# Heads of q and k turned by VectorE block transposes, stored in another column order and scaled by ScalarE

## The chip, the cores and the metric

The program runs on one core of a Trainium2 chip. The metric is the device time of one execution in microseconds (us), lower is better; the median of three runs stands for the kernel. The core has a matrix engine (PE, TensorE), a vector engine (DVE), a scalar engine (ACT), a general engine (POOL, GpSimd) and a queue engine (SP, SyncE) that only issues transfers. Each runs its own list of instructions in order and waits for others by semaphores.

## The reference, cut to what matters

Three layers stand one behind the other: a retention layer, a chunked attention layer and a mix of pooling and latent attention, on 1024 positions of width 1024. The change touches the second one:

```python
def chunked_attention_mixer(h, w_in, q_g, k_g, rel_table, w_out):
    proj = h @ w_in                                # 1024 x 8192: q, k, v, g, 16 heads of 128 each
    q, k, v, g = jnp.split(proj, 4, axis=-1)
    q = rms_norm_f32(q.reshape(B, S, 16, 128), q_g)   # norm over the 128 of a head
    k = rms_norm_f32(k.reshape(B, S, 16, 128), k_g)
    ...
    s = jnp.einsum('bqhd,bkhd->bhqk', q_j, k_j) * scale + bias    # 64 queries, 576 keys
    p = jax.nn.softmax(s, axis=-1)
    return jnp.einsum('bhqk,bkhd->bqhd', p.astype(v.dtype), v_j)
```

The scores contract over the 128 of a head, so PE wants q and k of a head with the head dimension on the partitions (turned), while the projection h @ w_in leaves positions on the partitions.

## The kernel before, in words

**Products.** All large products are float32 and are made of three passes of a rounded format (high by high, low by high, high by low; `product`, lines 1182 to 1184). The weights therefore pass a ring of RING = 4 slots: a raw tile in SBUF, then ACT copies its high part (`hi`, line 1813, into `w_hi`), then POOL subtracts to get the low part (line 1068, `w_lo`), then PE uses both. `hi(n)` waits until PE is done with slot n - 4, so at best it stands three slots ahead of its use.

**Blocks.** The input projection of the attention layer is cut in 16 blocks, numbers 12 to 27, and each block is computed with seven products (Strassen's scheme), whose left and right factors are sums. DVE forms the weight sums (`wide_sum` line 2386, raw sums line 2368) and adds the products from PSUM into four quadrants c11, c22, c21, c12 of the block (`wide_evict`, line 2406; `evict`). The buffers of the quadrants are called c11, u3 (c22), m1s (c21) and u2 (c12); names with _k are those of the second block of a pair. Blocks 19, 21, 23, 25 are q and each is computed together with the k block behind it (20, 22, 24, 26) as a "wide" pair: a slot of theirs feeds 256 columns of both and a product has four slots, in the order 0, 3, 1, 4, 5, 2, 6. Block 27 is v, not wide, with two slots in a product. So a wide pair is followed by a wide pair three times, and by block 27 once.

**Norm of q and k.** Behind each quadrant of a pair (128 x 1024 for q and as much for k) DVE squares (line 2470), reduces to 8 sums (line 2471), ACT takes the root (line 1892), DVE inverts (line 2477) and scales the whole buffer by one multiplication (`unit_scale`, line 2479). SP then stores it, one transfer of 512 KB with rows of 1 KB (line 687), to `blk` in HBM, positions by columns. The buffers are used again by the next pair: ACT's `m1s_copy` (line 1883) waits for the stores of c21, DVE's eviction u2 for those of c12.

**Attention.** It works in tiles e = 8 h + i (head h, 128 queries i). SP loads q, k and v of a head in runs of 512 B (`a_load`, line 964). PE turns q and k, four pieces of four 128 x 128 tiles to a head (`a_turn_head`, lines 1368 to 1377, at the tiles listed in `A_TURN_AT`; the four pieces of head 0 stand at product 5 of block 27), into PSUM; ACT writes the high part with the gain multiplied in (line 2105), DVE the low part (line 2841). Per tile PE computes scores (`a_scores`), turns the probabilities (`a_turn`, line 1522, ACT copies them out by lines 2132 to 2135) and multiplies by v (`a_values`, line 1534); DVE takes maxima, ACT the exponentials, DVE the inverse sum, POOL multiplies by it (line 1134). The stage runs from about 1484 us to 1760 us.

## Time and profile before

| | |
|---|---|
| median of 3 runs | 2449.77 us (2449.53 to 2451.17) |
| the profiled execution | 2450.25 us, its span 2448.4 us |
| mean granted TensorE clock | 0.999 |
| busy share PE, DVE, ACT, POOL | 99%, 64%, 45%, 50% |

The span is the stretch from the first to the last instruction on the chip. Where a row gives a start time, it is counted from the start of the span. Shares are means over all stages, which have different loads.

### The profile page before, as it was taken

Reading aid. Unit: us, or ns where it says so; the run is one execution under the profiler, and the core shown is the slowest. Engines: PE = TensorE matmul, PEld = TensorE weight load, DVE = VectorE, ACT = ScalarE, POOL = GpSimd, SP = SyncE. Lnnn points to the kernel's source line nnn. Section 1 sums busy time; section 2 is a strip of 40 time slices with the busy share of each in tenths; the row PEclk is TensorE's granted clock in tenths of the full one; section 3 lists DMA queues with packets and bytes.
Section 4 is the critical chain, followed back from the end, with each engine's and each line's share of the span. In section 5 each row is a group of like instructions: output and inputs, shape, how many; then the busy total and the mean of one; then the engine's idle time right before and its main releaser. Section 6 shows DMA issues by size and latency. Waiting matters only on the chain.

```text
span 2448.4 us, 36045 instructions
## 1 busy us (share of the span) xinstructions
PE 2419.0 (99%) x13808; PEld 2076.6 (85%) x13808; DVE 1578.4 (64%) x2151; ACT 1105.7 (45%) x2052; POOL 1235.7 (50%) x883
## 2 busy tenths in 40 slices
PE   7999999999999999999999999999999999999999
PEld 6888898875588898899888899999988888788887
DVE  6965657588543386653766766666434489788863
ACT  5322223344544353322322226777534434888861
POOL 1645545430044455545555555555454445866664
PEclk9999999999999999999999999999999999999999
DMA  7554544493034345543332257454144343300034
GB/s 277 157 190 154 180 163 158 142 325 137 27 112 156 104 150 181 176 142 107 122 116 98 89 166 226 124 156 121 50 135 158 105 161 123 103 1 1 2 127 156
DMA packets 241196, 329.21 MB, mean 134 GB/s; under 512 B 19401, under 2 KB 173825, under 8 KB 239233
## 3 DMA queue, kind: packets, MB, share of 16 engines
q1 hardware_dynamic: 239552, 326.80, 40.3%
q8 instruction: 111, 1.82, 0.3%
q14 instruction: 61, 0.49, 0.1%
q10 hardware_dynamic: 1472, 0.10, 0.0%
HBM read 247.53 MB, written 79.33 MB: 133 GB/s over the span
## 4 chain that ended last, share of the span: by engine, by line
PE 91%; DVE 5%; issue 2%; ACT 1%; POOL 1%; DMA 1%; SPq 0%; DVEq 0%; ACTq 0%
PE ps L1182 23%; PE ps L1184 23%; PE ps L1183 23%; PE ps L1534 4%; PE ps L1707 2%; PE ps L1522 2%; PE ps L1688 2%; PE ps L1451 2%; PE ps L1470 2%; PE ps L1464 1%; DVE s_raw L2349 1%; PE ps L1375 1%; PE ps L1202 1%; PE ps L1434 1%; PE ps L1407 1%
## 5 line engine op out<-in xcount | busy, mean ns | idle before, releaser
L1068 POOL TENSOR_TENSOR w_lo<-raw,w_hi 128x512 fp32r<-128x512 f32 (+1 forms) x452 | 652.9, 1453 | 794.4 <-ACT w_hi L1813 758.8
L1813 ACT ACTIVATE w_hi<-raw 128x512 fp32r<-128x512 f32 (+1 forms) x456 | 282.9, 629 | 795.1 <-PE ps L1184 633.4
L1182 PE MATMUL ps<-w_hi,s_hi 128*128 128x256 f32 (+2 forms) x832 | 262.8, 316 | 0.8 <-POOL w_lo L1068 0.3
L1183 PE MATMUL ps<-w_lo,s_hi 128*128 128x256 f32 (+2 forms) x832 | 262.0, 315 | 0.0
L1184 PE MATMUL ps<-w_hi,s_lo 128*128 128x256 f32 (+2 forms) x832 | 262.0, 315 | 0.0
L1068 POOL TENSOR_TENSOR w_lo<-raw_wide,w_hi 128x512 fp32r<-128x512 f32 x112 | 174.0, 1560 | 131.3 <-ACT w_hi L1813 131.3
L2462 DVE TENSOR_TENSOR u<-u,ps 128x1024 f32<-128x1024 f32 (+1 forms) x96 | 116.4, 1212 | 148.9 <-PE ps L1184 145.5
L1182 PE MATMUL ps<-w_hi,a_hi 128*128 128x256 f32 (+2 forms) x624 | 196.7, 315 | 0.0
L1183 PE MATMUL ps<-w_lo,a_hi 128*128 128x256 f32 (+2 forms) x624 | 196.6, 315 | 0.0
L1184 PE MATMUL ps<-w_hi,a_lo 128*128 128x256 f32 (+2 forms) x624 | 196.5, 315 | 0.0
L1182 PE MATMUL ps<-s_hi,w_hi 128*128 128x512 f32 x480 | 188.6, 393 | 3.2 <-DVE s_lo L2336 2.3
L1134 POOL TENSOR_TENSOR a_p<-a_p,st 128x640 f32<-128x640 f32 (+4 forms) x128 | 130.7, 1027 | 117.9 <-DVE st L2880 117.7
L1184 PE MATMUL ps<-s_hi,w_lo 128*128 128x512 f32 x480 | 186.9, 389 | 0.0
L1183 PE MATMUL ps<-s_lo,w_hi 128*128 128x512 f32 x480 | 186.8, 389 | 0.0
L2368 DVE TENSOR_TENSOR raw<-raw 128x1024 f32<-128x1024 f32 (+1 forms) x96 | 134.5, 1401 | 58.4 <-DMA raw<-in_w 56.3
L1182 PEld LDWEIGHTS ps<-w_hi,s_hi 128*128 128x128 f32 x832 | 158.5, 191 | 12.7 <-issue 2.2
L1184 PEld LDWEIGHTS ps<-w_hi,s_lo 128*128 128x128 f32 x832 | 158.6, 191 | 10.0
L1183 PEld LDWEIGHTS ps<-w_lo,s_hi 128*128 128x128 f32 x832 | 158.6, 191 | 9.9
L1813 ACT ACTIVATE w_hi<-raw_wide 128x512 fp32r<-128x512 f32 x112 | 70.5, 633 | 195.9 <-PE ps L1184 177.7
L1162 POOL TENSOR_TENSOR l_p<-l_p,st 128x1024 f32<-128x1024 f32 x64 | 121.3, 1895 | 72.9 <-DVE st L3056 71.8
L1182 PE MATMUL ps<-a_hi,w_hi 128*128 128x512 f32 x360 | 141.7, 393 | 0.0
L1183 PE MATMUL ps<-a_lo,w_hi 128*128 128x512 f32 x360 | 140.9, 391 | 0.0
(341 smaller groups left out, 6214.6 us busy)
## 6 DMA issues: line engine op xcount, KB each, us to landing
raw<-in_w SPq DMA_DIRECT2D x159, 512.0 KB, 4.3
ada_c<-in_ada SPq DMA_DIRECT2D x14, 2304.0 KB, 10.8
blk<-u SPq DMA_DIRECT2D x54, 512.0 KB, 4.0
raw_wide<-in_w SPq DMA_DIRECT2D x32, 512.0 KB, 4.6
blk<-c SPq DMA_DIRECT2D x27, 512.0 KB, 3.4
blk<-m1s SPq DMA_DIRECT2D x27, 512.0 KB, 3.3
ada_first<-in_ada SPq DMA_DIRECT2D x12, 768.0 KB, 16.0
r_g<-blk SPq DMA_DIRECT2D x8, 1024.0 KB, 9.4
```

Of the source, the lines that this page charges most:

```text
L1068: pool.tensor_tensor(w_ring(w_lo, n), w_source(n), w_ring(w_hi, n).bitcast(F32), ALU.subtract)\
L1134: pool.tensor_tensor(a_p[:, e % 4, 0:w], a_p[:, e % 4, 0:w], st[:, 172 + e % 4:173 + e % 4].to_broadcast([P, w]), ALU.mult).then_inc(a_pro ...
L1162: pool.tensor_tensor(l_p[e % 3][:, :], l_p[e % 3][:, :], st[:, 136 + e % 4:137 + e % 4].to_broadcast([P, S]), ALU.mult)\
L1182: pe.matmul(out, a_hi_, b_hi_, start=first, stop=False, skip_group_check=True)
L1183: pe.matmul(out, a_hi_, b_lo_, start=False, stop=False, skip_group_check=True)
L1184: return pe.matmul(out, a_lo_, b_hi_, start=False, stop=last, skip_group_check=True)
L1451: mm = pe.matmul(ps[:, 2 + k], r_kd[r_kept(e) % 2][:, k * P:(k + 1) * P], r_v[h % 2][:, i], start=(i != 1), stop=(i != 0))
L1470: mm = pe.matmul(ps[:, 4 + e % 2], r_q[h % 2][:, k, i * P:(i + 1) * P], r_state_at[b % 2][:, k], start=False, stop=(k == 1))
L1534: mm = pe.matmul(ps[:, 6 + i // 4, (i % 4) * P:(i % 4 + 1) * P], a_v[h % 4][:, j], a_pT[:, e % 2, c * P:(c + 1) * P], start=(c == 0), stop ...
L1813: act.activation(w_ring(w_hi, n), w_source(n), ACT.Copy).then_inc(w_rounded, 1)
L2368: dve.tensor_tensor(raw_quad(dst, s), raw_quad(left, s), raw_quad(right, s), ALU.subtract)\
L2462: dve.tensor_tensor(quad_tile(buf, s), quad_tile(base, s), product_banks(s, i), ALU.add)\
```

## The change

- **Column order.** The wide evictions write a quadrant so that, in each partition, the 1024 columns stand in the order (j, b, i): i the 32 columns of a block of 32, b the row block of 128 positions, j the block of 32 columns. The squares (line 2517) undo the order as they write, so that the reduction reads as before.
- **Scaling.** It goes from DVE to ACT: DVE still sums and inverts (`unit_inverse`, lines 2521 to 2528, both blocks of a pair together), and ACT multiplies in place, eight instructions of 128 x (4x32) for each buffer (`unit_scale`, lines 1920 to 1928), 16 for the two buffers of a pair's quadrant, 256 in all.
- **Turning.** DVE transposes the scaled buffer in place in blocks of 32 x 32, one instruction of 128 x 1024 (`unit_turn`, lines 2530 to 2534), 32 in all. The buffers are then stored by four transfers each (line 704), each of 32 partitions with runs of 512 B (128 KB), and q and k lie in HBM with columns by positions. `stored_count` counts four for each such quadrant.
- **Attention.** `a_load_qk` (line 994) loads rows of 4 KB on 128 partitions, already turned; v comes by `a_load_v` apart. PE's head turns and their positions are gone. ACT's high part (`a_head_high`, line 2142) and DVE's low part (line 2890) now read SBUF, in the old places (`A_SPLIT_AT`). The gain of k is multiplied into that of q, so k is split without a factor. q and k have two buffers instead of four; their load for the next head stands behind that of v and g in SP's order. In `(1, 0)` ACT waits for all stores of blocks up to 27 (before, DVE waited for two quadrants of them).
- **Smaller moves.** PE's wait for quadrant c21 of block 27 goes to the place before the first scores, at product 6, step 3. PE waits for v at the first tile of each head.

The diff, cut to its core:

```diff
@@ -677,6 +698,13 @@
+                if kind == "unit":
+                    for g in range(4):
+                        at = 512 * a + P * g
+                        sp.dma_start(turned_rows(s)[256 * c:256 * c + 256, at:at + P].rearrange("(j i) t -> i j t", i=32),
+                                     quad_buf(s, quad)[32 * g:32 * g + 32, :].rearrange("i (j t) -> i j t", t=P))\
+                            .then_inc(stored[quad], 16)
+                    return
...
+                def a_load_qk(h):
+                    n, c = h % 2, slice((h % 4) * P, (h % 4) * P + P)
+                    if h > 1:
+                        sp.wait_ge(a_hlow, 4 * (h - 1))
+                    for s, dst in ((AQ[h // 4], a_q), (AK[h // 4], a_k)):
                         in_memory(s)
-                        sp.dma_start(dst[n][:, :, :], rows_of(s)[:, c].rearrange("(m p) n -> p m n", p=P))\
-                            .then_inc(ah_in[n], 16)
+                        sp.dma_start(dst[n][:, :, :].rearrange("p m n -> p (m n)"), turned_rows(s)[c, :])\
+                            .then_inc(aqk_in[n], 16)
@@ -1293,6 +1335,7 @@
                         if (s, i, k) == (27, 6, 3):
+                            pe.wait_ge(ev, evicted(27, "c21"))
                             a_scores(0)
                             a_scores(1)
...
-            def a_turn_head(h, n):
-
-                if n == 0:
-                    pe.wait_ge(ah_in[h % 4], 48 * (h // 4 + 1))
-                if h:
-                    pe.wait_ge(a_hlow, 1 if (h, n) == (1, 0) else 4 * h + n)
-                for m in range(4):
-                    tr = pe.transpose(ps[:, a_piece_bank(h, n), m * P:(m + 1) * P],
-                                      a_half((a_q[h % 4], a_k[h % 4]), n)[:, m], ident[:, :])
-                tr.then_inc(a_hturned, 1)
@@ -1888,9 +1913,19 @@
+            def unit_scale(s, quad):
+
+                q, e, whole = QUADS.index(quad), s - wide_of(s), quad_buf(s, quad)
+                act.wait_ge(u_sums, inverse_count(s, quad))
+                heads = whole[:, :].rearrange("p (h f b i) -> p b h f i", h=2, f=4, b=4)
+                for m in range(8):
+                    part = heads[:, m // 2, m % 2]
+                    ins = act.activation(part, part, ACT.Identity, scale=u_st[e][:, 1, q, m:m + 1])
+                ins.then_inc(u_scaled, 1)
...
                     if p < 6 or s + 2 in WIDE:
                         hi(ahead + 2)
                         hi(ahead + 3)
+                    if quad and (p or s - 1 in UNIT):
+                        for e in range(2):
+                            unit_scale(s + e if p else s + e - 2, quad)
...
                         if i == 1 and s - 1 in UNIT:
                             post(s - 2, "c12")
                             post(s - 1, "c12")
+                            unit_scale(s - 2, "c12")
+                            unit_scale(s - 1, "c12")
@@ -2415,31 +2464,28 @@
                 wide_sum(s, 2)
                 if s - 1 in UNIT:
-                    unit_sums(s - 2, "c12")
-                    unit_sums(s - 1, "c12")
-                    unit_scale(s - 2, "c12")
-                    unit_scale(s - 1, "c12")
+                    unit_turn(s - 2, "c21")
+                    unit_turn(s - 1, "c21")
+                    unit_inverse(s - 2, "c12")
                 wide_sum(s, 1)
+                if s - 1 in UNIT:
+                    unit_turn(s - 2, "c12")
+                    unit_turn(s - 1, "c12")
...
+            def unit_turn(s, quad):
+
+                flat = quad_buf(s, quad)[:, :]
+                dve.wait_ge(u_scaled, unit_count(s, quad))
+                dve.transpose(flat, flat).then_inc(p_unit, 1)
...
                     k = A_PIECES[n][0]
-                    dve.scalar_tensor_tensor(a_half((a_qlo[h % 2], a_klo[h % 2]), n),
-                                             ps[:, a_piece_bank(h, n)].rearrange("p (m n) -> p m n", m=4),
-                                             gains[:, k:k + 1], a_half((a_qhi[h % 4], a_khi[h % 4]), n).bitcast(F32),
-                                             ALU.mult, ALU.subtract).then_inc(a_hlow, 1)
+                    if k:
+                        dve.tensor_tensor(a_turned(a_klo[h % 2], n), a_stored(a_k[h % 2], n),
+                                          a_turned(a_khi[h % 2], n).bitcast(F32), ALU.subtract).then_inc(a_hlow, 1)
+                        return
+                    low, raw_, high = a_turned(a_qlo[h % 2], n), a_stored(a_q[h % 2], n), a_turned(a_qhi[h % 2], n)
+                    for m in range(4):
+                        ins = dve.scalar_tensor_tensor(low[:, m], raw_[:, m], gains[:, k:k + 1], high[:, m].bitcast(F32),
+                                                       ALU.mult, ALU.subtract)
+                    ins.then_inc(a_hlow, 1)
```

The first place is ACT's list where pair 25/26 goes over into block 27. raw2 are weights of products 1 and 2 of block 27, the next raw0 and raw1 those of products 3 and 4; u_st and r_st are the statistics of the q and the k block. Before:

```order
L1813 ACTIVATE w_hi<-raw0 128x512 x2
L1892 ACTIVATE u_st<-u_st,eps 128x8
L1892 ACTIVATE r_st<-r_st,eps 128x8
L1813 ACTIVATE w_hi<-raw2 128x512 x4
L1883 ACTIVATE m1s<-ps 128x1024
L1892 ACTIVATE u_st<-u_st,eps 128x8
L1892 ACTIVATE r_st<-r_st,eps 128x8
L1813 ACTIVATE w_hi<-raw0 128x512 x2
L1813 ACTIVATE w_hi<-raw1 128x512 x2
```

and after:

```order
L1838 ACTIVATE w_hi<-raw0 128x512 x2
L1917 ACTIVATE u_st<-u_st,eps 128x8
L1917 ACTIVATE r_st<-r_st,eps 128x8
L1927 ACTIVATE m1s<-m1s,u_st 128x4x32 x8
L1927 ACTIVATE m1s_k<-m1s_k,r_st 128x4x32 x8
L1838 ACTIVATE w_hi<-raw2 128x512 x4
L1908 ACTIVATE m1s<-ps 128x1024
L1917 ACTIVATE u_st<-u_st,eps 128x8
L1917 ACTIVATE r_st<-r_st,eps 128x8
L1927 ACTIVATE u2<-u2,u_st 128x4x32 x8
L1927 ACTIVATE u2_k<-u2_k,r_st 128x4x32 x8
L1838 ACTIVATE w_hi<-raw0 128x512 x2
```

The 16 scalings of c21 (m1s, m1s_k) now stand ahead of the high parts for product 1, and the 16 of c12 (u2, u2_k) ahead of the high part for product 3.

The second place is DVE's list where one wide pair goes over into the next; u2 is c12 of the old pair and m1s its c21, raw_wide are weight sums of the new one. Before:

```order
L2406 TENSOR_TENSOR u2<-u2,ps 128x1024 [waits ev,w_used]
L2406 TENSOR_TENSOR u2_k<-u2_k,ps 128x1024
L2386 TENSOR_TENSOR raw_wide0<-raw_wide3,raw_wide4 128x2048 [waits raw_in3,w_split,sums_done]
L2470 TENSOR_TENSOR u_sq<-u2 128x1024 [waits u_sums,ev]
L2471 TENSOR_REDUCE u_st<-u_sq 128x8 [waits chain]
L2470 TENSOR_TENSOR u_sq<-u2_k 128x1024 [waits u_sums,ev]
L2471 TENSOR_REDUCE r_st<-u_sq 128x8 [waits chain]
L2477 RECIPROCAL u_st<-u_st 128x8 [waits u_roots]
L2479 TENSOR_TENSOR u2<-u2,u_st 128x1024 [waits chain]
```

and after:

```order
L2435 TENSOR_TENSOR raw_wide0<-raw_wide3,raw_wide4 128x2048 [waits raw_in3,w_split,sums_done]
L2534 STREAM_TRANSPOSE m1s<-m1s 128x1024 [waits u_scaled]
L2534 STREAM_TRANSPOSE m1s_k<-m1s_k 128x1024 [waits u_scaled]
L2517 TENSOR_TENSOR u_sq<-u2 128x8x4x32 [waits u_sums,ev]
L2518 TENSOR_REDUCE u_st<-u_sq 128x8 [waits chain]
L2517 TENSOR_TENSOR u_sq<-u2_k 128x8x4x32 [waits u_sums,ev]
L2518 TENSOR_REDUCE r_st<-u_sq 128x8 [waits chain]
L2528 RECIPROCAL u_st<-u_st 128x8 [waits u_roots]
L2528 RECIPROCAL r_st<-r_st 128x8 [waits u_roots]
L2435 TENSOR_TENSOR raw_wide1<-raw_wide3,raw_wide1 128x2048 [waits sums_done]
L2534 STREAM_TRANSPOSE u2<-u2 128x1024 [waits u_scaled]
L2534 STREAM_TRANSPOSE u2_k<-u2_k 128x1024 [waits u_scaled]
```

The turns of c21, which wait for ACT's scalings, came in ahead of the sums of c12, and the multiplications of c12 (L2479) gave place to turns that wait for ACT's scalings.

The third place is PE's list in the attention stage, head 0 and 1 of it. Before:

```order
L1522 MATMUL ps<-ident,a_p 128x128 [waits a_pevac,a_prob]
L1375 MATMUL ps<-ident,a_k2 128x128 [waits a_hlow]
L1375 MATMUL ps<-ident,a_k2 128x128 x3
L1534 MATMUL ps<-a_pT,a_v0 128x128 [waits a_pevac]
L1534 MATMUL ps<-a_pT,a_v0 128x128 x4
```

and after:

```order
L1547 MATMUL ps<-ident,a_p 128x128 [waits a_pevac,a_prob]
L1561 MATMUL ps<-a_pT,a_v0 128x128 [waits a_pevac]
L1561 MATMUL ps<-a_pT,a_v0 128x128 x4
L1224 MATMUL ps<-a_khi1,a_qhi1 128x384 [waits a_max]
L1225 MATMUL ps<-a_klo1,a_qhi1 128x384
```

The four head turns between the turns of the probabilities and the product with v are gone, so the values follow directly on the last turn.

## Rows read from the trace of the kernel before

**Rows 1.** The page, part 1: busy us, share of the span, instructions.
```profile
PE 2419.0 (99%) x13808; PEld 2076.6 (85%) x13808; DVE 1578.4 (64%) x2151; ACT 1105.7 (45%) x2052; POOL 1235.7 (50%) x883
```

**Rows 2.** Stretches: window, its us; busy PE, PEld, DVE, ACT, POOL; clock; DMA; GB/s.
```profile
1010.00:1430.00 420.00, 420.00 (x2182) 360.92 (x2181) 269.02 (x225) 119.76 (x202) 228.85 (x153) 1.00 0.36 121
...
1520.00:1600.00 80.00, 80.00 (x663) 78.93 (x662) 49.00 (x189) 60.82 (x152) 47.37 (x43) 1.00 0.55 153
```

**Rows 3.** PE's waits between 1000 and 1760 us: total us, times, longest.
```profile
PE ps L1522 <- POOL a_p L1134: 0.7, 1, 0.7
```

**Rows 4.** Chain of waits, 1425 to 1490 us: start, us, instructions.
```profile
1473.67 1.75 PE ps L1375 x16
```

**Rows 5.** Timeline of PE's weight loads: start us, us, instruction, count.
```profile
1561.32 0.47 PEld L1375 LDWEIGHTS ps<-ident,a_k 128*128 128x128 f32 x4
1561.76 1.20 PEld L1534 LDWEIGHTS ps<-a_pT,a_v 128*128 128x128 f32 x10
```

**Rows 6.** DVE by form: busy us, mean ns of one, idle before.
```profile
L2386 DVE TENSOR_TENSOR raw_wide<-raw_wide 128x2048 f32<-128x2048 f32 x16 | 40.6, 2535 | 0.2
...
L2471 DVE TENSOR_REDUCE u_st<-u_sq 128x8 f32<-128x1024 f32 x16 | 19.5, 1220 | 0.5
```

**Rows 7.** Timeline of ACT, retention layer: two in a row.
```profile
709.43 1.32 ACT L1864 ACTIVATE r_ohi<-r_g,gn_col 128x512 fp32r<-128x512 f32 x2
```

**Rows 8.** ACT by form: the same instruction over all.
```profile
L1864 ACT ACTIVATE r_ohi<-r_g,gn_col 128x512 fp32r<-128x512 f32 x32 | 21.2, 709 | 0.0
```

**Rows 9.** Timeline of ACT in the attention stage.
```profile
1568.48 0.28 ACT L2132 ACTIVATE a_pT<-ps 128x128 f32<-128x128 f32 x1 [0.47 <-PE ps L1522]
1568.65 0.59 ACT L2133 ACTIVATE a_pT<-ps 128x512 f32<-128x512 f32 x1
```

**Rows 10.** Timeline of DVE, one wide pair into the next.
```profile
1213.00 2.28 DVE L2386 TENSOR_TENSOR raw_wide<-raw_wide 128x2048 f32<-128x2048 f32 x1
1215.20 1.22 DVE L2470 TENSOR_TENSOR u_sq<-u 128x1024 f32<-128x1024 f32 x1
...
1217.78 2.13 DVE L2470 TENSOR_TENSOR u_sq<-u_k 128x1024 f32<-128x1024 f32 x1
1219.94 1.22 DVE L2471 TENSOR_REDUCE r_st<-u_sq 128x8 f32<-128x1024 f32 x1
```

**Rows 11.** Timeline of ACT in the same place.
```profile
1199.80 0.63 ACT L1813 ACTIVATE w_hi<-raw_wide 128x512 fp32r<-128x512 f32 x1 [2.09 <-PE ps L1184]
...
1222.45 1.00 ACT L1883 ACTIVATE m1s<-ps 128x1024 f32<-128x1024 f32 x1
...
1227.00 0.64 ACT L1813 ACTIVATE w_hi<-raw_wide 128x512 fp32r<-128x512 f32 x1 [1.73 <-PE ps L1184]
```

**Rows 12.** Timeline of POOL in the same place.
```profile
1205.95 1.30 POOL L1068 TENSOR_TENSOR w_lo<-raw_wide,w_hi 128x512 fp32r<-128x512 f32 x1 [1.36 <-ACT w_hi L1813]
```

**Rows 13.** Timeline of ACT, pair 25/26 into block 27.
```profile
1428.28 0.63 ACT L1813 ACTIVATE w_hi<-raw_wide 128x512 fp32r<-128x512 f32 x1 [2.08 <-PE ps L1184]
...
1439.16 0.63 ACT L1813 ACTIVATE w_hi<-raw 128x512 fp32r<-128x512 f32 x1 [1.75 <-PE ps L1184]
...
1456.43 0.63 ACT L1813 ACTIVATE w_hi<-raw 128x512 fp32r<-128x512 f32 x1 [2.17 <-PE ps L1184]
```

**Rows 14.** Timeline of DVE in the same place.
```profile
1441.48 5.00 DVE L2368 TENSOR_TENSOR raw<-raw 128x1024 f32<-128x1024 f32 x4
```

**Rows 15.** Transfers: count, KB each, median us from issue to landing.
```profile
blk<-u_k SPq DMA_DIRECT2D x8, 512.0 KB, 3.1
```

**Rows 16.** Timeline of ACT at the start of the attention stage.
```profile
1484.67 0.28 ACT L2135 ACTIVATE a_pT<-ps 128x128 f32<-128x128 f32 x1
```

**Rows 17.** Timeline of SP's queue at the same place.
```profile
1486.90 0.36 SPq L964 DMA_DIRECT2D a_q<-blk  x1
```

**Rows 18.** DVE by form, low parts: from two SBUF tiles, from PSUM.
```profile
L2602 DVE SCALAR_TENSOR_TENSOR r_olo<-r_g,gn_col,r_ohi 128x512 fp32r<-128x512 f32 x32 | 26.4, 877 | 17.2 <-ACT r_ohi L1864 17.2
...
L2841 DVE SCALAR_TENSOR_TENSOR a_klo<-ps,gains,a_khi 128x512 fp32r<-128x512 f32 x32 | 23.9, 746 | 9.4 <-ACT a_khi L2105 9.4
```

More of the change, by code:

```diff
@@ L170, in rows_of, with turned_rows, stored_count @@
             return blk[s][0:(512 if BLOCKS[s][1] == "F" else S) * width].rearrange("(t n) -> t n", n=width)
+        def turned_rows(s):
+            return blk[s][0:512 * S].rearrange("(n t) -> n t", t=S)
+        def stored_count(blocks):
+            return 16 * (blocks + 3 * sum(1 for u in UNIT if u < blocks))
         ident = sb("ident", [P, P])
@@ L754, in wide_block @@
                 early[s + 2]()
[L755 removed]
+                sp.wait_ge(stored["c22"], stored_count(s + 2))
                 load_raw(R22, s + 2)
@@ L1386, in a_scores @@
                 width = (i + 1) * P - lo
-                hi, low = (k[:, :, :].rearrange("p m n -> p (m n)") for k in (a_khi[h % 4], a_klo[h % 2]))
+                hi, low = (k[:, :, :].rearrange("p m n -> p (m n)") for k in (a_khi[h % 2], a_klo[h % 2]))
                 for c, end in ((0, 3 * P), (3 * P, width)) if width > 4 * P else ((0, width),):
-                    mm = product(psf[:, base + c:base + end], a_qhi[h % 4][:, i], a_qlo[h % 2][:, i],
+                    mm = product(psf[:, base + c:base + end], a_qhi[h % 2][:, i], a_qlo[h % 2][:, i],
                                  hi[:, lo + c:lo + end], low[:, lo + c:lo + end], True, True)
                 mm.then_inc(a_sdone, 1)
-            def a_entry(s, i):
-                if (s, i) == (27, 5):
-                    pe.wait_ge(ev, evicted(27, "c21"))
-                    for n in range(4):
-                        a_turn_head(0, n)
             pe.wait_ge(c_ready, 1)
@@ L1510, in _ @@
             if LAST > 0:
-                projections(1, a_entry)
+                projections(1)
                 def a_turn(e):
@@ L2397, in wide_evict @@
                 if free:
-                    dve.wait_ge(stored[free], 16 * s)
+                    dve.wait_ge(stored[free], stored_count(s))
                 for e in range(2):
@@ L2425, in wide_block @@
                 wide_evict(s, "c11")
+                unit_inverse(s, "c11")
+                wide_evict(s, "u3")
                 for e in range(2):
-                    unit_sums(s + e, "c11")
-                for e in range(2):
-                    unit_scale(s + e, "c11")
-                wide_evict(s, "u3")
+                    unit_turn(s + e, "c11")
                 if s + 2 in WIDE:
@@ L2433, in wide_block @@
                 wide_evict(s, "c22")
-                for e in range(2):
-                    unit_sums(s + e, "c22")
-                for e in range(2):
-                    unit_scale(s + e, "c22")
+                unit_inverse(s, "c22")
                 wide_evict(s, "c21")
                 for e in range(2):
-                    unit_sums(s + e, "c21")
-                for e in range(2):
-                    unit_scale(s + e, "c21")
+                    unit_turn(s + e, "c22")
+                unit_inverse(s, "c21")
             def evict(s, what):
@@ L2454, in evict @@
                 if free:
-                    dve.wait_ge(stored[free], 16 * s)
+                    dve.wait_ge(stored[free], stored_count(s))
                 if what in ("c11", "u2"):
@@ L2550, in projections @@
                     if before:
-                        unit_sums(s - 2, "c12")
-                        unit_sums(s - 1, "c12")
+                        unit_turn(s - 2, "c21")
+                        unit_turn(s - 1, "c21")
+                        unit_inverse(s - 2, "c12")
                     if piece is not None:
```

142 lines of the change are left out of this document (82 added, 60 removed).

## The prediction

> **What bounds the kernel now.** I read the busy shares first: PE is busy 99% of the span [rows 1]. Then, per stage, the stretches: in the projections of the wide pairs (1010 to 1430 us) and in the attention stage (1520 to 1600 us) PE is busy for the whole stretch, at the full granted clock [rows 2]; in the second, ACT has 60.8 of 80 us of work, in the first only 119.8 of 420. Then PE's waits: one of 0.7 us in 760 us [rows 3]. So whatever leaves PE shortens the time until another engine is late; whatever makes a high or low weight part late by more than its lead costs in full. That lead is three slots: a slot of a wide pair is 2.72 us, one of block 27 is 2.88 (its `hi` at 1439.16 and the one six slots on at 1456.43, [rows 13]).
>
> **Part 1, PE's head turns go.** The four pieces of head 0 (16 tiles, in product 5 of block 27) stand in the chain for 1.75 us [rows 4]. The other 15 heads have 60 pieces of four turns; the weight loads of one piece begin at 1561.32 and those of the next work at 1561.76 [rows 5], 0.44 us. 60 x 0.435 = 26.1, with 1.75 that is **-27.9 us**, all of it where PE has no wait.
>
> **Prices of the new work.** DVE's in-place transpose of 128 x 1024 is nowhere in the trace. Lower bound and nearest row: a pass over 128 x 1024 takes 1.22 us, as the reductions do; upper: a pass over twice the elements, 2.54 [rows 6]. I take one pass, 1.15 us from start to start (1.22 with its tail), since it reads and writes each element once. The Trainium skill ("Vector Engine (DVE) Microarchitecture Reference", section 3.8 on the transpose) says that it sustains one element per cycle per lane; no run here shows it yet, and by it the price would be that of the pass taken. ACT's short scaling (128 columns, a factor for each partition): the same form 512 wide takes 1.32 us for two, 0.71 for one [rows 7, 8], so 0.61 from start to start; a column costs 0.83 ns (0.59 us against 0.28 for 384 more columns, [rows 9]; 0.81 with the tail), so 0.61 - 384 x 0.00083 = 0.29. Lower bound: copies from PSUM of 128 columns follow each other in 0.17 [rows 9]. I take 0.29 as the same form: 16 in a row, 4.6 us, where DVE took 2 x 1.4. The square and the sum of a quadrant of a pair take 5.0 us (1.25 for each of four) [rows 6, 10], as before; one square beside POOL took 2.13 [rows 10].
>
> **Part 2, wide pair into wide pair (three times).** I follow the first. ACT may scale c22 after its `hi` at 1199.80 [rows 11]: 1200.4 to 1205.0; DVE turns it by 1206.2, sums c21 by 1211.2 (1207 before). Two due `hi` until 1212.5, c21 scaled by 1217.1. DVE evicts c12 from 1211.6, weight sum (2.28 with the wait for the slot, [rows 10]) until 1216.9, turns c21 by 1219.3 and sums c12 by 1224.3; that ended at 1221.1 before [rows 10]. Then ACT: root and the two `hi` behind it to 1225.7, scaling of c12 to 1230.3, the two copies of m1s at 0.95 each [rows 11] to 1232.2, the next `hi` 1232.8, its low part on POOL 1.3 [rows 12] to 1234.2. Before, this `hi` stood one slot ahead of the one at 1227.00 [rows 11], so its slot was free at 1224.3 and PE wants it three slots later, at 1232.4. Stall 1.8 us; 2.7 if one square is stretched as above. I take 2.2, **+6.6 us** for three (0 to 6 each: 0 with short scalings at 0.17, 6 with two-pass transposes).
>
> **Part 3, pair 25/26 into block 27 (once).** Here a product is half as long and the scalings stand directly ahead of wanted high parts. c22 scaled 1428.9 to 1433.5 (behind the `hi` at 1428.28, [rows 13]), turned 1434.7, c21 summed 1439.7, scaled 1440.0 to 1444.6, then the first `hi` of product 1 to 1445.2 and POOL to 1446.6. Its slot was free at 1439.1 - 2.88, so PE wants it at 1444.7: stall 1.9. Then DVE: the last of the four weight sums (1.25 each, [rows 14]) waits for POOL's split of product 1 and ends at 1449.1, c21 turned by 1451.4, c12 summed by 1456.4; the stores of c21 land at about 1455.6 (issue 0.4, 3.1 to landing, [rows 15]); copy and roots to 1457.3, c12 scaled by 1461.9, `hi` of product 3 1462.5, POOL 1463.9. It is wanted at 1456.3 + 1.9 = 1458.2: stall 5.7. Together 7.6, 8.5 with a stretched square; I take **+8.0 us** (4 to 13).
>
> **Part 4, into the attention stage.** PE's wait for c21 of block 27 is passed long before; but the first scores now want low parts that DVE makes from SBUF, q in four instructions: +1.0 (-0.5 to 1.5). ACT's wait for all stores of block 27 stands in its list at 1484.95 [rows 16]; SP had passed the same wait by 1486.90 at the latest [rows 17], so up to 2 us and the exponentials queue behind it: +1.5 (0 to 3).
>
> **Part 5, attention with less PE work.** The stage runs from 1484 to 1760, so a head took 276 / 16 = 17.2 us; without 1.75 it is 15.4. ACT's 76% [rows 2] become 60.8 / 80 x 17.2 / 15.4 = 85%, with waits that were PE's shadow. DVE's low parts cost more: the form with two SBUF tiles takes 877 ns, that from PSUM 746 [rows 18], and q's has four starts. Covered while ACT and DVE are not late; I take +1.5 for places with 5 x 128 wide tiles (0 to 8). Loads of q and k now stand behind those of v and g, but have a head's time: 0. That DVE's scaling passes (two SBUF inputs, beside which POOL is slow) go is off the path: 0.
>
> **The sum.** -27.9 + 6.6 + 8.0 + 1.0 + 1.5 + 1.5 = **-9.3 us**. The profiled execution took 2450.25 us with a span of 2448.4, the median is 2449.77, 0.5 less; the same difference is taken from either: 2440.95 and **2440.5 us**. All low ends give -27.9 + 0 + 4 - 0.5 = -24.4 (2425); all high ends -27.9 + 18 + 13 + 1.5 + 3 + 8 = +15.6 (2465), which is not likely at once.
>
> **Rivals.**
> *A, short scalings cost 0.18 us* (the nearest bound for 128 columns, [rows 9]; against it: that row reads PSUM and has no factor). 16 take 2.9. Part 2 becomes 0.1 each, part 3 0.2 + 4.0 = 4.2: -27.9 + 0.3 + 4.2 + 4.0 = -19.4, **2430.4**. 20%.
> *B, all is covered*, part 3 too, because DVE and ACT idle more than I follow: -27.9 + 2, **2424**. 8%.
> *C, slower: the transposes take two passes*, 2.54 instead of 1.15 us [rows 6]. Three of them lie on each chain (one of c22, two of c21): 3 x 1.39 = 4.2 at each of four transitions, +16.7: +7.4, **2457.2**. It decides from 1.15 + 9.3 / 12 = 1.93 us on. For it: nothing in the trace moves data across partitions on DVE. 12%.
> *D, attention keeps half of its time*: ACT's 85% come in lumps (exponentials of 640, then copies), and half of the 26.1 comes back as PE waits for ACT: -9.3 - 1.5 + 13.1 = +2.3, **2452**. For it: the one wait now is for this chain [rows 3]; against it: only one. 12%.
> *E, the quarter stores are slow.* 128 KB from 32 partitions in runs of 512 B, four for one. If the stores of c21 land 6.5 us later than I take (twice 3.1 for each of two buffers), ACT stands at the copy of m1s ahead of c12's scaling in part 3 and PE waits 6.5 more; in part 2 ACT reaches that copy only at 1230.3, 11 us after the turn, and nothing is lost: -2.8, **2447**. 8%. The Trainium skill ("SBUF — State Buffer", section "Door 1: The DMA port swizzle") has a rule for this: a transfer over 32 partitions reaches 8 of the 16 ports, and two at once do not add up. By its figures (189 against 328 GB/s) a buffer's stores would take 5.4 us instead of 3.1, an estimate; no row of before has such a transfer.
>
> **How the numbers follow.** The forecast has 40%, the rivals 20, 8, 12, 12 and 8. About 0.2%, 4.9 us, is what a measurement of this kernel can tell from no change; so faster is below 2444.9, slower above 2454.7. Faster: 36 of the forecast's 40, A, B, and 1 each of D and E: 66. Same: 4 + 9 of D + 6 of E + 2 of C: 21. Slower: 10 of C, 2 of D, 1 of E: 13. The range 2424 to 2455 leaves out C, and some 6 of the edges of B, D and E.
>
> **What would show it.** Turning rows gone from PE and a head in 15.4 us (attention 1485 to 1733) prove part 1; 17 us and waits of `ps` for ACT or POOL prove D. The transpose's mean against 1.22 and 2.54 decides C; the mean and the pitch of the 128 x (4x32) scalings 0.29 against 0.18 decides A. PE's waits for POOL `w_lo` should stand at three places with 2.2 us (near 1232) and in two at block 27, 1.9 and 5.7 us; none there means B. ACT's wait ahead of `m1s` for DMA in block 27 means E. It is wrong outside of all these if the squares and evictions in the new column order cost more than 1.25 us each, or if PE waits in the middle of a wide pair, where I take the scalings (16 x 0.29 in a product of 10.9 us) as hidden.

## The result, and the profile after

The changed kernel takes **2462.51 us** (median of 4, 2461.11 to 2463.52) against 2449.65 (2449.39 to 2451.17): 0.5% slower, ratio 1.005 with an interval of 1.0037 to 1.0063. The forecast was 2440.5, the range ended at 2455. The profiled execution took 2463.52 us; its page begins:

```profile
span 2461.7 us, 35994 instructions
PE 2403.2 (98%) x13552; PEld 2055.0 (83%) x13552; DVE 1613.6 (66%) x2247; ACT 1174.8 (48%) x2308; POOL 1219.0 (50%) x883
```

PE has 256 instructions less than in [rows 1] and waits more. Its waits from 1000 to 1800 us (total us, times, longest), to be read against the single one of [rows 3]:

```profile
PE ps L1224 <- POOL w_lo L1110: 19.4, 6, 7.5
PE ps L1547 <- POOL a_p L1176: 5.3, 10, 0.9
PE ps L1224 <- DVE a_klo L2894: 1.4, 2, 1.0
PE ps L1547 <- ACT a_pT L2181: 1.2, 1, 1.2
```

**Where they stand.** The timeline of PE: three waits of 3 us where a wide pair follows on a wide pair, and two in block 27.

```profile
1231.17 0.64 PE L1224 MATMUL ps<-w_hi,s_hi 128*128 128x512 f32 x1 [3.00 <-POOL w_lo L1110]
1231.61 0.63 PE L1225 MATMUL ps<-w_lo,s_hi 128*128 128x512 f32 x1
...
1235.14 0.39 PE L1225 MATMUL ps<-w_lo,s_hi 128*128 128x512 f32 x1
...
1393.43 0.50 PE L1224 MATMUL ps<-w_hi,s_hi 128*128 128x512 f32 x1 [3.08 <-POOL w_lo L1110]
...
1462.40 0.36 PE L1224 MATMUL ps<-w_hi,a_hi 128*128 128x256 f32 x1 [2.56 <-POOL w_lo L1110]
...
1483.25 0.55 PE L1224 MATMUL ps<-w_hi,s_hi 128*128 128x256 f32 x1 [7.49 <-POOL w_lo L1110]
```

Behind most of them the matmuls are slow for 3 to 4 us (0.43 from start to start instead of 0.23 for 512 columns, 0.21 instead of 0.12 for 256), and the granted clock of the stretches (window, its us, busy us of PE, PEld, DVE, ACT, POOL, then PEclk) shows why: it fell from 2.4 GHz to the level of 1.2 for part of them.

```profile
1230.00:1240.00 10.00, 8.83 (x32) 7.13 (x33) 3.90 (x4) 7.31 (x18) 6.64 (x6) 0.83 0.47 105
...
1392.00:1402.00 10.00, 8.31 (x35) 6.60 (x36) 3.86 (x4) 7.58 (x19) 6.66 (x6) 1.00 0.48 106
...
1482.00:1492.00 10.00, 8.75 (x58) 8.78 (x59) 1.43 (x2) 4.07 (x7) 6.29 (x6) 0.73 0.99 268
```

Four of the five long waits were followed by such a stretch; the one at 1393, as long as the others, was not.

**The sum of the profiled runs.** Against before, DVE's copy of c11 out of PSUM, which follows PE at once, is 1.2 us late in the first pair (1168.37 against 1167.16: the start of the program), 15.0 in the last (1410.60 against 1395.64). Before, then after:

```profile
1167.16 1.23 DVE L2402 COPY c<-ps 128x1024 f32<-128x1024 f32 x1 [6.33 <-PE ps L1184]
...
1395.64 1.22 DVE L2402 COPY c<-ps 128x1024 f32<-128x1024 f32 x1 [6.33 <-PE ps L1184]
```

```profile
1168.37 1.23 DVE L2451 COPY c<-ps 128x1024 f32<-128x1024 f32 x1 [6.33 <-PE ps L1226]
...
1410.60 1.22 DVE L2451 COPY c<-ps 128x1024 f32<-128x1024 f32 x1 [5.16 <-PE ps L1226]
```

So the three changes of pair cost 13.8 us (4.9, 5.0, 3.9). PE's product with v in the attention stage starts 28.7 us later than before (1514.8 against 1486.1), though the turns of head 0 (1.75) are gone: block 27 costs 28.7 + 1.75 - 15.0 = 15.5. From the first to the last of these products it took 253.9 us, before 269.2 (before, then after):

```profile
L1534 PE MATMUL ps<-a_pT,a_v x960: 275/275/377, 1486.1 to 1755.3; 128*128 128x128 f32 x192
...
L1561 PE MATMUL ps<-a_pT,a_v x960: 273/275/377, 1514.8 to 1768.7; 128*128 128x128 f32 x192
```

That is -15.3 instead of the -26.1 of the turns: 10.8 lost. 1.2 + 13.8 + 15.5 - 1.75 - 15.3 = +13.4, and the spans differ by 13.3.

**The new operations by form** (DVE and ACT; busy us, mean ns of one, idle before):

```profile
L2534 DVE STREAM_TRANSPOSE u_k<-u_k 128x1024 f32<-128x1024 f32 x8 | 10.0, 1247 | 8.7 <-ACT u_k L1927 8.7
...
L2899 DVE SCALAR_TENSOR_TENSOR a_qlo<-a_q,gains,a_qhi 128x128 fp32r<-128x128 f32 x128 | 45.7, 416 | 18.6 <-ACT a_qhi L2155 18.6
L2894 DVE TENSOR_TENSOR a_klo<-a_k,a_khi 128x512 fp32r<-128x512 f32 x32 | 32.9, 1028 | 9.5 <-ACT a_khi L2152 9.5
```

The transpose is a pass, 1.25 us (1.16 from start to start). Eight scalings on ACT take 2.43 us, so 0.29 each from start to start (the last row of the next fence). The low parts of q and k cost far more than in [rows 18]: 45.7 and 32.9 us for 32 pieces each, against 24.

**Between two pairs.** ACT's timeline, which answers to [rows 11], with POOL's row for the low part that PE waited for:

```profile
1219.10 1.14 ACT L1838 ACTIVATE w_hi<-raw_wide 128x512 fp32r<-128x512 f32 x2
1224.70 0.30 ACT L1917 ACTIVATE u_st<-u_st,eps 128x8 f32<-128x8 f32 x1 [4.47 <-DVE u_st L2518]
1227.29 0.30 ACT L1917 ACTIVATE r_st<-r_st,eps 128x8 f32<-128x8 f32 x1 [2.28 <-DVE r_st L2518]
1227.49 1.14 ACT L1838 ACTIVATE w_hi<-raw_wide 128x512 fp32r<-128x512 f32 x2
1228.54 2.43 ACT L1927 ACTIVATE u<-u,u_st 128x128 f32<-128x128 f32 x8
```

```profile
1228.19 4.17 POOL L1110 TENSOR_TENSOR w_lo<-raw_wide,w_hi 128x512 fp32r<-128x512 f32 x2 [5.85 <-ACT w_hi L1838]
```

The third high part of the product stands behind the roots of c12 and so behind DVE's sums, which the turn of c21 pushed back; the same place was in my chain with 1225.7 and I followed it past, to the high part behind the scaling.

**Into block 27.** DVE waited for a weight load that SP had put behind five loads of the attention stage, and then ACT for the stores of c21, ahead of the roots, the scaling and the wanted high parts. The load was issued at 1454.59 and landed 9.2 us later (its row: count, KB, us to landing). Of the three sums that stood behind it only the last one had to wait for POOL's low parts, which were done at 1463.5:

```profile
raw<-in_w SPq DMA_DIRECT2D x1, 512.0 KB, 9.2
```

```profile
1460.99 2.50 POOL L1110 TENSOR_TENSOR w_lo<-raw,w_hi 128x512 fp32r<-128x512 f32 x2 [8.30 <-ACT w_hi L1838]
```

```profile
1463.84 3.75 DVE L2417 TENSOR_TENSOR raw<-raw 128x1024 f32<-128x1024 f32 x3 [4.50 <-DMA raw<-in_w]
```

```profile
1474.98 1.02 ACT L1908 ACTIVATE m1s<-ps 128x1024 f32<-128x1024 f32 x1 [6.21 <-DMA blk<-m1s_k]
...
1481.15 2.17 ACT L1838 ACTIVATE w_hi<-raw 128x512 fp32r<-128x512 f32 x4
```

### The profile page after: what moved, and what is told of

The parts are those of the page before. It is cut to its first block, busy times and chain, and to the rows that moved or that the text cites. A ratio compares the mean times of both kernels' runs of the same rounds, so it can differ in the third digit from the quotient of the medians.

```text
span 2461.7 us, 35994 instructions
## 1 busy us (share of the span) xinstructions
PE 2403.2 (98%) x13552; PEld 2055.0 (83%) x13552; DVE 1613.6 (66%) x2247; ACT 1174.8 (48%) x2308; POOL 1219.0 (50%) x883
## 4 chain that ended last, share of the span: by engine, by line
PE 83%; DVE 7%; ACT 3%; issue 2%; DMA 2%; POOL 1%; SPq 0%; DVEq 0%; ACTq 0%
PE ps L1224 22%; PE ps L1225 22%; PE ps L1226 22%; PE ps L1561 4%; PE ps L1732 2%; PE ps L1713 2%; PE ps L1547 2%; PE ps L1476 2%; PE ps L1495 2%; PE ps L1489 1%; DVE s_raw L2398 1%; POOL w_lo L1110 1%; PE ps L1244 1%; PE ps L1459 1%; DVE u_sq L2517 1%
## 5 line engine op out<-in xcount | busy, mean ns | idle before, releaser
L1110 POOL TENSOR_TENSOR w_lo<-raw_wide,w_hi 128x512 fp32r<-128x512 f32 x112 | 163.9, 1476 | 155.2 <-ACT w_hi L1838 155.2
L1226 PE MATMUL ps<-a_hi,w_lo 128*128 128x512 f32 x360 | 140.4, 390 | 0.0
```

Source lines behind the costliest of these rows:

```text
L1110: pool.tensor_tensor(w_ring(w_lo, n), w_source(n), w_ring(w_hi, n).bitcast(F32), ALU.subtract)\
L1226: return pe.matmul(out, a_lo_, b_hi_, start=False, stop=last, skip_group_check=True)
```

## The experiments

Each run is compared with the median of the kernel before that was taken together with it (2449.70, 2450.03, 2449.83 or 2450.37); the changed kernel is 12.9 us above its own. "Less" and "more" are counted from the changed kernel's 2462.51.

**1. ACT's order alone.** In ACT's list:

```diff
-last product of a pair: hi, hi, roots c21, hi, hi, scale c21 (16)
+last product of a pair: hi x4, roots c21
-hi, hi, roots c12, hi, hi, scale c12 (16), copy m1s (2), hi x4
+hi, scale c21 (8), hi, scale c21 (8), hi, hi, roots c12
+hi, scale c12 (8), hi, copy m1s (2), hi, scale c12 (8), hi
-block 27: hi x2 (product 2), copy m1s, roots c12, scale c12 (16), hi x2 (product 3)
+block 27: hi x2 (product 2), hi x2 (product 3), copy m1s, roots c12, scale c12 around the hi of product 4
```

The scalings of c11 and c22 also stand between single high parts now, and in block 27 so do those of c21, at product 1.

> The changed kernel with ACT's list alone reordered: no high part of a weight stands behind a root or a whole scaling that is due later; the two scalings of a pair's quadrant stand between single high parts, and the copy of m1s stands behind two high parts of its product. Theory 1 (the three stalls of 3.0 us between wide pairs come from a high part that stands behind a root that waits for DVE, and each costs 4.8 us with the half clock behind it): the three go, -14.4 us, and the two of block 27 (2.6 and 7.5 us) shrink, -5 to -10; 2438 to 2443 us. Theory 2 (DVE is the late one: its weight sums come late because of the turns ahead of them, whatever ACT does): PE waits stay within 3 us of 14.6 in sum, 2455 us or more.

Measured: 2449.85 us, ratio 1.000 (0.9991 to 1.001), 12.7 less than the changed kernel and between the two theories' ranges. PE's waits:

```profile
PE ps L1224 <- ACT m1s_k L1908: 7.6, 3, 2.8
PE ps L1547 <- POOL a_p L1176: 5.3, 10, 0.9
PE ps L1224 <- POOL w_lo L1110: 2.0, 1, 2.0
```

The 7.5 us of block 27 are gone by order alone. Between the pairs the wait for the low part became one for the copy of m1s. That copy may not start before c21 is stored, but in ACT's timeline it doesn't wait for a store here: it stands behind the roots, which wait for DVE's sums of c12, and behind the first scaling of c12.

```profile
1230.14 0.30 ACT L1917 ACTIVATE r_st<-r_st,eps 128x8 f32<-128x8 f32 x1 [2.28 <-DVE r_st L2544]
...
1233.73 1.00 ACT L1908 ACTIVATE m1s<-ps 128x1024 f32<-128x1024 f32 x1
```

So theory 1 holds for block 27. For the pairs there is a second bound right behind the first, and it comes from the same round trip between DVE and ACT.

**2. Roots behind the high parts, and nothing else.**

```diff
-hi, hi, roots c12, hi, hi, scale c12
+hi, hi, hi, hi, roots c12, scale c12
```

> The changed kernel with one move in ACT's list, between two wide pairs only: the two roots of c12 stand behind the four high parts of the next product instead of between the second and the third. Theory 1 (the third high part is late because it stands behind a root that waits for DVE's sums): the three waits for the low part of 3.0 us go; the copies of m1s end 1 us later than PE wants their bank, so a wait of 0 to 1 us is left: 3 times 4 to 4.8 us less, 2448 to 2451 us. Theory 2 (the high part is late because DVE's weight sum is): the waits stay at 3 us and the time within 2 us of the changed kernel.

Measured: 2465.03 us (1.0058, interval 1.0044 to 1.0072). The wait of 3.0 us at the third high part is gone in all three places, and one of 3.4 stands a few slots on, behind the scaling and the copies:

```profile
1236.46 0.47 PE L1224 MATMUL ps<-w_hi,a_hi 128*128 128x512 f32 x1 [3.42 <-POOL w_lo L1110]
```

Theory 1 was right on the cause of the first wait and wrong on the gain. The changed kernel had hidden the second one, which is the one of part 2 of the prediction, behind the first: there that low part was ready at 1237.0, and PE, held up by the first wait and the slow matmuls behind it, came to it only at 1238.3.

**3. DVE scales.** Two instructions of 512 columns for each buffer, behind the inverse; ACT scales nothing.

```diff
+                heads = quad_buf(s + e, quad)[:, :].rearrange("p (h f b i) -> p h b f i", h=2, f=4, b=4)
+                for n in range(2):
+                    dve.tensor_tensor(heads[:, n], heads[:, n], root[:, n] (broadcast to 4x4x32), ALU.mult)
```

> The changed kernel with the scaling back on DVE, right behind the inverses, as two instructions of 512 columns for each buffer; the turns stay where they are, ACT scales nothing. Theory 1 (the round trip DVE, ACT, DVE and ACT's 4.7 us for a pair hold up both lists): the three stalls between wide pairs go (-14.4) and c22 is stored about 5 us earlier, so block 27 loses half of its 14.6: about 2441 us. Theory 2 (DVE has no room for 2.6 us more at each quadrant of a pair): weight sums come later than now and PE waits as long as in the changed kernel or longer, 2460 us or more.

Measured: 2456.21 us (1.0026, 1.0016 to 1.0035), 6.3 less. The three waits are 2.6 us instead of 3.0; in block 27 the 7.5 became 1.2, behind one of 2.75. So neither theory holds as it stands: taking the scaling off ACT helps in block 27, and between the pairs the third high part still stands behind a root that waits for DVE's sums (the root at 1227.84, the high part at 1228.05). That the order decides there is shown by run 10.

**4. The same with the weight load of block 27 ahead of the attention's.**

```diff
-                early[s + 2]()
                 sp.wait_ge(stored["c22"], stored_count(s + 2))
                 load_raw(R22, s + 2)
+                early[s + 2]()
```

> The run dve_scales with one more edit in SP's list: the weight load that DVE's second sum for block 27 waits for (4.5 us in the changed kernel) stands ahead of the five loads for the attention stage instead of behind them. If that wait is on the path to the stores of c21 and so to PE's stall of 7.5 us, 2 to 5 us less than dve_scales; if the stall has its end set by ACT's and DVE's work alone, the same within 1 us.

Measured: 2455.47 us (1.0023, 1.0014 to 1.0033), 0.7 less than run 3, which is within their spread. The wait in block 27 went from 2.75 to 2.08 us, and DVE's wait for the load, 0.69 us in run 3, is gone. So there was little to win in run 3. This doesn't clear the load in the changed kernel, where DVE waited 4.50 us for it; it was not moved there alone.

**5. One transfer for four.** Runs of 2 KB, 128 partitions. q and k then lie in HBM in another order than the attention stage reads; this part of the computation is changed, the work of the engines is the same.

> The changed kernel with one transfer from 128 partitions for each turned buffer instead of four from 32 (runs of 2 KB; the places in HBM are others, this part of the computation is changed). Rival E of the prediction (the quarter stores hold up the copy of m1s): in block 27 the copy waits for the store for 6.2 us in the changed kernel and PE 7.5 us; from the end of the turn to landing 5.1 us there, some 3.5 with one transfer, so the PE wait shrinks by 1 to 2 us, 2460 to 2461.5 us. If four transfers from 32 partitions were slow as such, by more: 3 us or more. If landing is hidden: no change.

Measured: 2461.62 us (1.0048, 1.0033 to 1.0064), 0.9 less, which is within the spread; the wait of 7.5 us became 6.7:

```profile
1480.21 0.55 PE L1222 MATMUL ps<-w_hi,s_hi 128*128 128x256 f32 x1 [6.69 <-POOL w_lo L1108]
```

```profile
blk<-u_k SPq DMA_DIRECT2D x32, 128.0 KB, 2.5
```

The second row is of the changed kernel (its transfers: count, KB, median us to landing). A quarter lands 2.5 us after its issue begins, and SP issues four in 1.9 us, so a buffer takes some 3.9 us; one transfer took 3.4 in this run (3.1 before, [rows 15]). For the two buffers of c21 in block 27 it is 6.2 us from the first issue to the start of the copy in the changed kernel and 4.5 here. Less than 1 us of this reaches PE, because ACT then stands for DVE's sums of c12:

```profile
1473.23 0.30 ACT L1915 ACTIVATE r_st<-r_st,eps 128x8 f32<-128x8 f32 x1 [1.38 <-DVE r_st L2516]
```

Rival E, which had 6.5, is worth under 1 us.

**6. q's low part once.** ACT and DVE leave q in stored order, so the queries of a tile are permuted.

```diff
-                    for m in range(4):
-                        ins = dve.scalar_tensor_tensor(low[:, m], raw_[:, m], gains[:, k:k + 1], high[:, m].bitcast(F32),
+                    dve.scalar_tensor_tensor(low, raw_, gains[:, k:k + 1], high.bitcast(F32),
```

> The changed kernel with the high and low parts of q left in the order in which they are stored, so that DVE makes the low part in one instruction of 512 columns instead of four of 128. PE reads them as if turned, so the queries of a tile are permuted (this part of the computation is changed). Theory 1 (in the attention stage DVE, busy 80%, is what PE waits for through the maxima, the inverse and POOL's product; 10.8 of 26.1 us are lost so): 32 times 0.8 us less on DVE, 4 to 7 us regained, 2456 to 2458 us. Theory 2 (ACT, busy 81%, is the late one): within 1.5 us of the changed kernel, 2461 to 2463.

Measured: 2458.91 us (1.0037, 1.0024 to 1.005), 3.6 less; the attention stage takes 250.2 us from first to last product with v, 3.7 less. One instruction takes 0.94 us on average (30.1 us for 32), the four together 1.43.

**7. The low parts left out** but for 32 columns of each piece, from head 2 on.

```diff
+                    if h > 1:
+                        dve.tensor_tensor(low[:, 0:1, 0:1], raw_[:, 0:1, 0:1], high[:, 0:1, 0:1], ALU.subtract)
+                        return
```

> The changed kernel with the low parts of heads 2 to 15 left out but for 32 columns in each piece (this part of the computation is left out). DVE's share in the attention stage falls from 80% to about 55%, ACT's and POOL's work stays. Theory 1 (the low parts from SBUF on DVE are all of the lost time): the stage shrinks by up to 10 us and the waits for POOL's product go, 2452 to 2454 us. Theory 2 (ACT at 85% sets the rest): after the 3.6 us that one instruction for q gave back, little more: 2457 to 2459.

Measured: 2454.87 us (1.0018, 1.0008 to 1.0028), 7.6 less. The stage takes 245.3 us, 8.6 less, and in 1600 to 1700 PE never waits. That stretch, first of the changed kernel, then of this run:

```profile
1600.00:1700.00 100.00, 97.73 (x788) 95.27 (x785) 80.15 (x292) 81.09 (x203) 62.77 (x56) 1.00 0.48 159
```

```profile
1600.00:1700.00 100.00, 100.00 (x823) 98.69 (x822) 65.00 (x265) 83.73 (x213) 64.66 (x59) 1.00 0.46 153
```

ACT is busier than ever at 84% and PE is full: of the 10.8 us lost in the stage, 8.6 are DVE's low parts. The trace of the changed kernel shows 1.6 of the other 2.2, all at the start: 0.4 is PE's wait for a low part of head 1, and 1.2 is one wait for ACT's copy of the turned probabilities (1517.28). ACT was late there because it had stood 1.8 us for the stores of block 27, which is the second item of part 4 (+1.5):

```profile
1515.44 0.72 ACT L2155 ACTIVATE a_qhi<-a_q,gains 128x512 fp32r<-128x512 f32 x1 [1.79 <-DMA blk<-u]
```

**8. The low parts behind the maxima.**

```diff
-                    if e - 2 in A_SPLIT_AT: a_head_low
                     a_maxima(e + 2)
                     a_inverse(e + 1)
+                    if e - 2 in A_SPLIT_AT: a_head_low
```

> The changed kernel with one reordering on DVE in the attention stage: the low part of a piece (q 4 x 128 columns, k 512) stands behind the maxima of tile e + 2 and the inverse of tile e + 1 instead of ahead of them. The work is the same. Theory 1 (what costs time there is that the dearer low parts stand in front of the maxima, in the chain from scores to the turned probabilities): most of the waits for POOL's product go, 4 to 8 of the 10.8 us lost there come back, 2455 to 2459 us. Theory 2 (DVE's load as such, or ACT): within 1.5 us of the changed kernel.

Measured: 2476.3 us (1.0108, 1.0093 to 1.0124), 13.8 more than the changed kernel. The waits for POOL's product went, as theory 1 had it, and 16 waits for the low parts came, up to 1.7 us, one at each head's first scores:

```profile
PE ps L1224 <- POOL w_lo L1110: 20.3, 7, 7.5
PE ps L1224 <- DVE a_klo L2894: 12.6, 16, 1.7
```

The low parts have no room to go back, and the same instructions also took longer at their new place: q's four 2.08 us instead of 1.43, k's one 0.78 instead of 1.03, together 12.8 us more on DVE.

```profile
L2899 DVE SCALAR_TENSOR_TENSOR a_qlo<-a_q,gains,a_qhi 128x128 fp32r<-128x128 f32 x128 | 66.6, 579 | 0.0
```

Which of the two costs the 13.8 us was not separated. Neither theory came out, and **both_mended**, this order on top of run 9, lands at 2466.77 (1.0069, 1.0056 to 1.0082), 13.9 above run 9, as far as here:

> proj_mended and low_last together. The two places are apart in time, so their gains should add: proj_mended less what low_last gains on the changed kernel, 2428 to 2433 us, faster than the kernel before by 0.7 to 0.9%. If either gain is given back elsewhere, it lands above 2437.

**9. The projections mended.** Runs 3 and 4, and: roots of c21 and c12 behind the high parts, product 3's high parts ahead of the copy in block 27, c21 turned right behind its scaling.

> The changed kernel with the projections mended by what the runs act_hi_first and dve_scales showed: DVE scales (two instructions for a buffer), c21 is turned right behind its scaling where a wide pair follows, so that its store lands before the copy of m1s is due; in ACT's list no high part stands behind a root at the two ends; the second weight load of block 27 stands ahead of the attention's loads. If holding m1s and the order of the high parts are the two causes, no PE wait of over 1 us between 1190 and 1480 us, so 29 us less than the changed kernel less what DVE is now late: 2434 to 2438 us. If DVE's own load sets the end (its 9.9 us for each quadrant of a pair), waits for weight sums of 2 us or more at each transition remain and it lands at 2445 or above.

Measured: 2452.85 us (1.0013, 1.0004 to 1.0022), 9.7 less than the changed kernel and 15 above the upper end of what was expected. Three waits of 2.65 us for a low part are left between the pairs and one of 2.1 in block 27. ACT shows what is late now:

```profile
1221.88 2.19 ACT L1838 ACTIVATE w_hi<-raw_wide 128x512 fp32r<-128x512 f32 x4 [10.10 <-DVE raw_wide L2437]
```

The weight sum had moved back with the turn ahead of it.

**10. The work of run 9 in another order on DVE.** In block 27, all four weight sums also stand ahead of the eviction of c12, and in ACT's list product 4's high parts ahead of the copy.

```diff
 sums, scale c22
-evict c21; turn c22; sums, scale c21; turn c21; evict c12; weight sum; sums, scale c12; weight sum; turn c12
+turn c22; evict c21; sums, scale c21; weight sum; evict c12; turn c21; sums, scale c12; turn c12; weight sum
```

> proj_mended with DVE's list at the ends of a pair in another order: c22 is turned before c21 is evicted, and the weight sum that the next high parts wait for stands ahead of the eviction of c12, the turn of c21 and the sums of c12; in block 27 all four weight sums stand ahead of them and the high parts of products 3 and 4 ahead of the copy of m1s. The work on each engine is that of proj_mended. If the stalls of 2.7 us there (high parts 10.1 us behind a weight sum) come from the order alone, no PE wait over 1 us is left between 1190 and 1480 us and the time falls by three times 4.4 and 3.5, 17 us: 2435 to 2439 us. If DVE has too much work between the eviction of c22 and the copy's or the eviction's due time, a wait of PE for an eviction or a copy takes its place: 2445 or above.

Measured: **2437.47 us**, ratio 0.9952 (0.9937 to 0.9967): 15.4 less than run 9 by order alone, 25 less than the changed kernel and faster than before. Between 1190 and 1430 PE has no wait, with DVE at 85% (first the changed kernel, then this one):

```profile
1190.00:1430.00 240.00, 230.65 (x1000) 189.30 (x999) 162.81 (x143) 116.81 (x306) 123.16 (x84) 0.99 0.36 95
```

```profile
1190.00:1430.00 240.00, 240.00 (x1061) 198.72 (x1060) 204.39 (x204) 66.25 (x120) 125.03 (x89) 1.00 0.39 103
```

DVE has 42 us more work here and the pairs lose nothing: c11 of one pair stands 76.2 us behind that of the last, as before. So it was never DVE's load.

**11. k's low part on POOL**, heads 1 to 15, on top of run 10.

> proj_again with the low parts of k of heads 1 to 15 on POOL, behind its product for tile e, at tiles e - 2 of the split list; q stays on DVE. DVE has 2.1 us less for each head, POOL 2.6 us more (64% to 80%). If DVE alone is what PE waits for (low_short gave back 8.6 us with all low parts gone), 3 to 6 us less than proj_again: 2431 to 2434 us. If POOL, which stands in the same chain (its product is what PE waits for), is as late as DVE was, no gain or a loss: 2437 or above.

Measured: 2461.88 us (1.0048, 1.0035 to 1.0062), 24 above run 10. Waits for POOL's product went from 5.3 to 13.1 us, and before the scores PE stands 14 times for something that the profile doesn't name; the one wait added there is that for POOL's low parts. So the second of the two cases came: POOL is as late as DVE was.

```profile
PE ps L1560 <- POOL a_p L1185: 13.1, 17, 2.0
PE ps L1235 <- issue: 11.2, 14, 1.5
```

## Why the prediction was wrong

**Right.** Part 1 (-27.9 us of PE work: a head without waits runs in 15.4 us in run 7, 1.75 less than the 17.15 before); the prices (0.29 us for a scaling, 1.16 for a transpose), so rivals A and C fall, though C's 2457.2 is the number nearest to the result; the places, three between pairs and two in block 27; in part 4, the first scores' wait (1.0, measured 1.04) and that of ACT (1.5, measured 1.2); E is small.

**The step that failed first: the stalls were sized too short and priced at their own length.** Part 2 took 2.2 us for each, part 3 8.0 for two. PE waited 3.0 each and 2.56 + 7.49, and a lower clock came on top: 4.9, 5.0 and 3.9 us lost at the pairs, 15.5 in block 27. Of the 29.3 us some 19 are wait for low parts, 1 the first scores' wait for theirs (as part 4 had it), and most of the other 9 the clock behind them: four stretches that lost 1.4 to 2 us each. Parts 2 and 3 and the first item of part 4 said 6.6 + 8.0 + 1.0 = 15.6.

**Second, in part 2, the wrong late place.** I costed the high part behind c12's scaling; the earlier one, behind the roots, was late too. In my chain it was ready at 1225.1 and its low part 1.3 later, with the 1.2 us of the start 0.6 before PE stopped at 1228.2. In the trace one square of each pair lasted longer (1.77 and 2.17 us instead of 1.25), so the high part came at 1228.1, and POOL's pass beside DVE's next weight sum took 2.9 us. Run 2 shows both waits one after the other.

**Third, in part 3, a load that the chain left out.** c21 landed at 1474.9 in the trace, where my chain with the delay of 15 us so far has 1470.6; ACT stood 6.2 us at the copy. Most of these 4.3 us arise ahead of the turn of c21: the weight sums ended at 1467.5 instead of 1464.1. Without the load DVE's last sum could have begun behind POOL's low parts, at about 1463.8, and ended at 1465.0, so by the trace 2.5 us are the load's, which part 3 had at nothing; no run moved it alone. The stores added 0.9: 5.1 us from the end of the turn to landing instead of 4.2. DVE's sums of c12 stand behind the same load and ended at 1475.8, so the stores alone hold up little (run 5). Run 1 shows that the order of ACT's list decides what of all this reaches PE: with the high parts ahead of the copy, the wait of 7.5 is gone though the copy still waits 5.2. A small slip besides: PE wants the first low part of part 3 at 1439.1 + 2 x 2.88 = 1444.9, not 1444.7, so that stall should read 1.7 and not 1.9.

**Fourth, part 5: +1.5 us, measured +9.6** (10.8 lost in the stage, less the 1.2 of ACT's wait, which is part 4's). This was rival D's place, by another engine. D named ACT; runs 6 and 7 show DVE. I took 0.13 us more for a low part from the 877 ns of [rows 18] and wrote of four starts without pricing them; q's piece costs 1.43 us (45.7 us for 32) instead of 0.75, of which the four starts are 0.49 (run 6: 0.94 for one instruction), and k's 1.03. That is 31 us more on DVE (45.7 + 32.9 against 2 x 23.9), which went from 61% [rows 2] to 80% in the stage.

So the mechanisms were mostly on paper and three terms were mis-sized in the same direction: +6.6 was 13.8; +8.0 and the 1.0 of the first scores were 15.5; +1.5 and the 1.5 of ACT's wait were 10.8. The forecast had -27.9 + 6.6 + 8.0 + 4.0 = -9.3; the runs show -27.9 + 13.8 + 15.5 + 10.8 + 1.2 = +13.4 (the last is the start of the program, and part 4 is in the 15.5 and the 10.8). The first stays inside its bound of 18, the second passes its 13 + 1.5, and the third comes close to its 8 + 3. The sum of all high ends, 2465, which I called not likely, is nearly what came.

The Trainium skill ("SBUF — State Buffer", section "Door 1: The DMA port swizzle") would, by the prediction's estimate from its figures, have had a buffer's quarter stores 2.3 us later. Here they are about 0.5 us later (3.9 against 3.4 in run 5), with 2.5 us for a transfer of 128 KB from 32 partitions. The figures are for transfers of 1 MiB; at 128 KB the estimate doesn't hold, and the measurement decides. "Vector Engine (DVE) Microarchitecture Reference", section 3.8, of the Trainium skill, agrees with the trace: transposes of 1024 elements a lane follow each other in 1.16 us, about as DVE's copies of that width do (1.14, from 1168.37 to 1169.51).

## What to carry to other kernels

When work moves onto an engine that also feeds the bottleneck, write down for each item the time at which it is wanted and put the ones wanted first ahead in its list; here the same work in another order was 15.4 us apart (runs 9 and 10). A chain that crosses to another engine and back in the middle of such a list holds up everything behind it, so follow each item of the list, not only the last. Price a stall of the matrix engine with what the clock takes after it, and price an instruction in its new shape and with its new neighbours, not by the form it replaces.
